# A fused hybrid-mixer and mixture-of-experts layer: the fourth head's projection order, its output-weight split, and the products of the recurrence's first and last step

## What is computed

```python
def step(S, inp):
    qg_c, kd_c, u_c, w_c, intra_c, a_c = inp
    v_new = u_c - jnp.einsum('bhik,bhkv->bhiv', w_c, S)
    o_c = (jnp.einsum('bhik,bhkv->bhiv', qg_c, S)
           + jnp.einsum('bhij,bhjv->bhiv', intra_c, v_new))
    S = S * a_c[..., None, None] + jnp.einsum('bhik,bhiv->bhkv', kd_c, v_new)
    return S, o_c
S0 = jnp.zeros((B, H, DK, DV), q.dtype)
_, o = lax.scan(step, S0, xs)
```

## Time and profile before

| what | us |
|---|---|
| median of 3 runs | 1310.05 |
| profiled execution | 1305.95 |
| its span, first to last instruction | 1304.1 |
| TensorE busy | 1246.6 (96% of the span) |
| head 3, from its gk round (462.43) to the end of rz6 | 72.61 |
| the same stretch of head 2 (337.46) | 60.38 |

### The profile page before, as it was taken

How to read it: one execution, slowest core, us unless ns; L and a number is a source line. 1 busy time by engine, 2 the same in 40 slices (tenths; PEclk the granted TensorE clock), 3 DMA queues, 4 the chain that set the end, 5 groups by cost and what they waited for, 6 DMA issues and landing times.

```text
span 1304.1 us, 25780 instructions
## 1 busy us (share of the span) xinstructions
PE 1246.6 (96%) x10894; PEld 1075.7 (82%) x10894; DVE 896.9 (69%) x1085; ACT 722.7 (55%) x919; POOL 174.1 (13%) x144
## 2 busy tenths in 40 slices
PE   7999999999999997899978999999999999999977
PEld 6989899989999997678877888888888888888854
DVE  7655457445655554324457889888989899889867
ACT  7351336133413432433235788878887878888834
POOL 0020111021102010600011111111111111111000
PEclk9999999999999998899988999999999999999998
DMA  7101010111010103045417999999999999999986
GB/s 212 50 17 36 18 46 21 36 34 33 29 27 31 33 18 131 2 189 182 178 50 278 375 377 392 383 390 394 395 386 378 394 385 390 388 381 384 371 333 256
DMA packets 38217, 273.98 MB, mean 210 GB/s; under 512 B 8163, under 2 KB 8419, under 8 KB 25844
## 3 DMA queue, kind: packets, MB, share of 16 engines
q1 hardware_dynamic: 28484, 251.67, 51.2%
q0 software_dynamic: 9216, 16.80, 3.4%
q10 hardware_dynamic: 432, 4.27, 0.9%
HBM read 260.11 MB, written 29.36 MB: 222 GB/s over the span
## 4 chain that ended last, share of the span: by engine, by line
PE 87%; DVE 7%; issue 2%; DMA 2%; ACT 2%; SPq 0%; DVEq 0%; POOLq 0%
PE bank L602 13%; PE bank L604 13%; PE bank L603 13%; PE bank L1317 8%; PE bank L1319 8%; PE bank L1318 8%; PE bank L489 2%; PE bank L493 2%; PE bank L491 2%; PE bank L593 2%; DVE arena L1887 1%; PE bank L1433 1%; PE bank L621 1%; PE bank L1460 1%; PE bank L1463 1%
## 5 line engine op out<-in xcount | busy, mean ns | idle before, releaser
L968 DVE TENSOR_TENSOR w_lo<-w_raw,w_hi 128x2048 fp32r<-128x2048 f32 x192 | 432.6, 2285 | 39.0 <-ACT w_hi L749 38.2
L749 ACT ACTIVATE w_hi<-w_raw 128x2048 fp32r<-128x2048 f32 x192 | 360.6, 1916 | 71.6 <-DMA w_raw<-in_w_up 46.8
L1317 PE MATMUL bank<-xn_hi,p_hi 128*128 128x364 f32 (+1 forms) x672 | 230.4, 343 | 4.8 <-DVE xn_lo L1834 2.5
L1319 PE MATMUL bank<-xn_hi,p_lo 128*128 128x364 f32 (+1 forms) x672 | 216.0, 321 | 0.0
L1318 PE MATMUL bank<-xn_lo,p_hi 128*128 128x364 f32 (+1 forms) x672 | 215.7, 321 | 0.0
L602 PE MATMUL bank<-w_hi,xgT_hi 128*128 128x512 f32 x512 | 206.3, 403 | 2.9 <-DVE xgT_lo L1026 2.9
L604 PE MATMUL bank<-w_hi,xgT_lo 128*128 128x512 f32 x512 | 201.4, 393 | 0.0
L603 PE MATMUL bank<-w_lo,xgT_hi 128*128 128x512 f32 x512 | 200.9, 392 | 0.0
L1317 PEld LDWEIGHTS bank<-xn_hi,p_hi 128*128 128x128 f32 x672 | 127.0, 189 | 7.7 <-DVE xn_lo L1834 2.8
L1318 PEld LDWEIGHTS bank<-xn_lo,p_hi 128*128 128x128 f32 x672 | 127.2, 189 | 0.3
L1319 PEld LDWEIGHTS bank<-xn_hi,p_lo 128*128 128x128 f32 x672 | 126.8, 189 | 0.0
(11 more groups left out here) (268 smaller groups left out, 1890.4 us busy)
## 6 DMA issues: line engine op xcount, KB each, us to landing
w_raw<-in_w_down SPq DMA_DIRECT2D x32, 2048.0 KB, 10.0
w_raw<-in_w_gate SPq DMA_DIRECT2D x31, 2048.0 KB, 10.9
w_raw<-in_w_up SPq DMA_DIRECT2D x31, 2048.0 KB, 9.9
p_raw<-in_w_tiles SPq DMA_DIRECT2D x28, 512.0 KB, 3.6
arena<-y_rows SPq DMA_DIRECT2D x8, 1024.0 KB, 13.7
arena<-in_tokens SPq DMA_DIRECT2D x10, 416.0 KB
w_out_raw<-in_w_out SPq DMA_DIRECT2D x4, 1024.0 KB, 9.4
arena<-in_tokens SPq DMA_DIRECT2D x8, 512.0 KB, 4.5
```

The lines of the kernel that those rows point to most:

```text
L749: nc.scalar.activation(w_hi[m][:, half], wraw[m if raw is None else raw][:, half], ACT.Copy).then_inc(hi_done[m], 1)
L968: nc.vector.tensor_tensor(w_lo[m][:, half], wraw[m if raw is None else raw][:, half], w_hi[m][:, half].bitcast(F32), ALU.subtract).then_in ...
L1317: nc.tensor.matmul(out[:, 0:n], p_hi[slot][:, k, :], hi, start=(k == 0), stop=False)
L1319: m = nc.tensor.matmul(out[:, 0:n], p_lo[slot][:, k, :], hi, start=False, stop=(k == KD - 1))
```

## The change

Four edits:

1. Head 3 gets the order of projection pieces of the other heads, on TensorE and VectorE. Its splits of y stand at other rounds.
2. `w_out` is therefore read later in the head (the wait for the last GB piece is the same). The split of its eight blocks is spread: two high parts on ScalarE behind ttr5, two behind the "mix" norm, four in steps 0 to 3; low parts of blocks 0, 2, 5, 3 on GpSimd, and of 1, 4, 6, 7 on VectorE.
3. The recurrence leaves out, in step 0, the products with the zero state (L1493, L1500) and VectorE's r, takes bv in r's place, and copies the first state; in step 9 it leaves out the product and the update of a state that nobody reads. The state's memset goes.
4. The gaps of a step are filled by `step_fill`: heads 0 to 2 get the next head's first Z piece in the gaps of step 9 (1, 2 and 5 of its 8 blocks) instead of behind it; head 3 gets its 18 units in steps 1 to 9, and none before the recurrence or in step 0.

```diff
+        HI_ORDER, LO_POOL, LO_DVE = [0, 1, 2, 4, 5, 6, 3, 7], [0, 2, 5, 3], [1, 4, 6, 7]
@@ TensorE
+            STEP_TILES = ([{1: range(2, 5), 2: range(5, 8)}] + [{0: range(0, 3), 1: range(3, 5), 2: range(5, 8)}] * (NC - 2)
+                          + [{0: range(0, 1), 1: range(1, 3), 2: range(3, 8)}])
             def scan(h, last):
-                if last:
-                    early_pair(0, 0)
-                else:
+                if not last:
                     fill(h, Q, 0, range(0, 2))
...
+                def step_fill(c, third):
+                    if last and c:
+                        early_pair(c - 1, third)
+                    if not last and third in STEP_TILES[c]:
+                        if c < NC - 1:
+                            fill(h, Q + c // 3, c % 3, STEP_TILES[c][third])
+                        else:
+                            fill(h + 1, Z, 0, STEP_TILES[c][third])
...
+                    if c:
+                        pe.wait_ge(s_done, h * (NC - 1) + c)
+                        nc.tensor.matmul(bank[3][0:C, 0:128], chunk(kT, c), state, start=True, stop=True).then_inc(ks_done, 1)
+                        step_fill(c, 0)
+                        if c >= 2:
+                            pe.wait_ge(osq_done, h * NC + c - 1)
+                        nc.tensor.matmul(o, state, chunk(qg, c), start=True, stop=False)
+                        pe.wait_ge(r_done, h * (NC - 1) + c)
+                    nc.tensor.matmul(bank[4][0:C, 0:128], rT[0:C, c, :], r_sb[0:C, :] if c else bv[0:C, 0, :],
                                      start=True, stop=True).then_inc(vnp_done, 1)
+                    step_fill(c, 1)
                     pe.wait_ge(vn_done, h * NC + c + 1)
+                    m = nc.tensor.matmul(o, vn_sb[0:C, :], dTi[0:C, c, :], start=(c == 0), stop=True)
+                    if c < NC - 1:
+                        m = nc.tensor.matmul(bank[6][:, 0:128], kd[0:C, c, :], vn_sb[0:C, :], start=True, stop=True)
+                    m.then_inc(ods_done, 1)
+                    step_fill(c, 2)
...
-                if last:
-                    fills = {"z1": [(GC, 2), (UU, 0)], "rz1": [(UU, 1), (UU, 2)], "z2": [(GB, 0), (GB, 1)], "rz2": [(GB, 2)]}
-                else:
-                    fills = {...}
+                fills = {"z1": [(GC, 2)], "rz1": [(UU, 0)], "ttr1": [(UU, 1, LOW)], "z2": [(UU, 1, HIGH)],
+                         "rz2": [(UU, 2, LOW)], "ttr2": [(UU, 2, HIGH)], "z3": [(GB, 0, LOW)], "rz3": [(GB, 0, HIGH)],
+                         "ttr3": [(GB, 1, LOW)], "z4": [(GB, 1, HIGH)], "rz4": [(GB, 2)]}
...
-                fill(h + 1, Z, 0)
                 scan_end(h)
@@ ScalarE
+                    if last and n == 3:
+                        early_high(2)
+                    if last and n == 4:
                         early_high(0)
-                    if last and n >= 3:
-                        for k in ((0, 1), (2, 3, 4), (5, 6, 7))[n - 3]:
...
+                    if last and n == 5:
+                        w_out_high(0)
+                        w_out_high(1)
                 log_exp_tables()
                 norm(h, "mix", 1.0 / 64, eps)
+                if last:
+                    w_out_high(2)
+                    w_out_high(3)
                 for c in range(NC):
                     act.wait_ge(vnp_done, h * NC + c + 1)
                     nc.scalar.activation(vn_sb[0:C, :], bank[4][0:C, 0:128], ACT.Copy).then_inc(vn_done, 1)
+                    if last and c < 4:
+                        w_out_high(c + 4)
@@ VectorE, in the recurrence
+                    if last and c in (1, 2, 5):
+                        w_out_low({1: 4, 2: 6, 5: 7}[c])
...
+                    if c == 0:
+                        nc.vector.tensor_copy(state, bank[6][:, 0:128]).then_inc(s_done, 1)
@@ GpSimd
+                    w_out_low(0)
+                    w_out_low(2)
...
                 for c in range(NC):
+                    if last and c in (1, 4):
+                        w_out_low(5 if c == 1 else 3)
```

More of the change, by code:

```diff
@@ L1491, in scan @@
                     o = bank[(5, 7)[c % 2]][:, 0:C]
[L1492 to L1499, removed]
@@ L1503, in scan @@
+                    nc.tensor.matmul(bank[4][0:C, 0:128], rT[0:C, c, :], r_sb[0:C, :] if c else bv[0:C, 0, :],
                                      start=True, stop=True).then_inc(vnp_done, 1)
[L1504 to L1507, removed]
+                    step_fill(c, 1)
                     pe.wait_ge(vn_done, h * NC + c + 1)
-                    nc.tensor.matmul(o, vn_sb[0:C, :], dTi[0:C, c, :], start=False, stop=True)
@@ L2039, in mixer @@
                 grp(h, "z1")
-                if last:
[L2041 to L2047, removed]
-                    early_low(1)
[L2049 to L2073, removed]
+                grp(h, "rz1")
+                u_piece(0)
+                grp(h, "z2")
+                lo_part(0, use(h, GB))
+                grp(h, "rz2")
+                if last:
+                    early_low(1)
+                u_piece(1)
+                grp(h, "z3")
+                u_piece(2)
+                grp(h, "rz3")
+                mix_conv()
+                gb_piece(0)
+                grp(h, "z4")
+                gb_piece(1)
+                grp(h, "rz4")
+                gb_piece(2)
                 if not last:
                     lo_part(SLOT[Q], use(h, Q))
+                if last:
+                    early_low(2)
                 for n in (5, 6):
@@ L2078, in mixer @@
                     grp(h, f"rz{n}")
+                    if last and n == 5:
+                        early_low(0)
+                if last:
+                    w_out_low(1)
                 if not last:
@@ L2112, in mixer @@
                 if not last:
-                    dve.wait_ge(s_done, h * (NC + 1) + NC + 1)
+                    dve.wait_ge(s_done, (h + 1) * (NC - 1))
                     head_copies(h + 1)
@@ L2139, in _, with w_out_low @@
             g_incl(0)
+            def w_out_low(k):
+                pool.wait_ge(wo_hi_done, HI_ORDER.index(k) + 1)
+                nc.gpsimd.tensor_tensor(w_out_lo[:, k, :], w_out_raw[:, k, :], w_out_hi[:, k, :].bitcast(F32),
+                                        ALU.subtract).then_inc(wo_lo_done, 1)
             def mixer(h, last):
@@ L2152, in mixer @@
                 if last:
-                    for k in range(KD):
-                        pool.wait_ge(wo_hi_done, k + 1)
-                        nc.gpsimd.tensor_tensor(w_out_lo[:, k, :], w_out_raw[:, k, :], w_out_hi[:, k, :].bitcast(F32),
-                                                ALU.subtract).then_inc(wo_lo_done, 1)
+                    w_out_low(0)
+                    w_out_low(2)
                 if not last:
```

41 lines of the change are left out of this document (22 added, 19 removed).

## The result

The changed kernel takes 1289.96 us (median of 5 runs, 1286.68 to 1293.68) against 1310.31 us (5 runs, 1308.07 to 1312.9): ratio 0.984, 95% interval 0.982 to 0.986, so 20.4 us less. The profiled execution took 1287.59 (span 1285.7) against 1305.95 (1304.1), 18.4 less, and that difference can be followed through the trace. The other 2.0 lie between the medians and the two profiled executions, and no trace shows them. By the interval of the ratio the changed kernel takes 1286.5 to 1292.5, so the run itself doesn't place it clearly outside the range.

What follows compares the result with a forecast made beforehand. It took TensorE to bound the kernel, idle or low-clocked in head 3. Gains 7.2 and 12.2 less 2.0 (gate), 0.2 (rest of head 3), 1.0 (port), 2.0 (clock) gave 14.2 us: 1296, range 1290.5 to 1301.5.

Steps and rivals of the forecast that it cites:

- Heads 0 to 2: Recurrence steps 0 and 9: dropped products and the Z fill save 2.4 us a head, 7.2 for three.
- Head 3's preparation: Head 3, gk round to rz6: with head 2's order it takes head 2's time, 12.2 us saved.
- instructions not yet there: Reading of TensorE's "issue" waits, up to 4.05 us, in head 3's dense small rounds beside a saturated DMA.
- Gate: Head 3, rz6 to step 1: output-weight landing and ScalarE's splits delay the recurrence, 7.1 us instead of 5.1, loss 2.0.
- against what I listed: Expected sign ahead of head 3's recurrence: ScalarE waits about 1 us for DMA before the first weight split.
- Clock: Head 3 near step 0: idle TensorE's clock falls to 0.50 for about 5 us, loss 2.0, ends 0 and 4.
- Port: Head 3, steps 1, 2 and 4: GpSimd and VectorE splits block each other, loss 1.0 us, ends 0 and 3.
- so I let a shift of head 3's end pass to the end unchanged: Behind head 3: output and expert products follow, so time gained there reaches the kernel's end in full.
- the experts' span unchanged: Expected sign behind head 3: the experts take as long as before the change.

Runs made afterwards that it cites:

- warm: The kernel gate plus 14 dummy products of 384 columns in TensorE's gaps ahead of step 0 and in steps 0 and 1; 1291.85 us, ratio 0.985.
- gate: The changed kernel with ScalarE's output-weight splits moved behind the first vn copies and early output products a step later; 1287.35 us, ratio 0.983.
- best: The kernel warm plus 17 float32 dummy products of 8 columns ahead of the first load's landing; 1288.04 us, ratio 0.981.

## Why the prediction was right, and where it failed

**Heads 0 to 2:** 7.2 forecast, 7.55 measured. The shares differ: dead products alone 1.5, Z beside step 9 1.05 once they are gone. Head 2's preparation gained waits on issue of 0.59 and 1.14 (gk to rz6 60.79 instead of 59.54), for which I had no term.

**Head 3's preparation:** 12.2 forecast, 12.5 measured. Reading it off head 2 was right, and "instructions not yet there" as the meaning of issue was right. What I blamed, the saturated DMA, is the smaller part: the transfer's place is worth 5.4, the order 8.7. The Trainium skill's "mostly hidden" (Runtime: NRT & Kernel Launch, "Instruction fetch mechanics"), which I set against the trace, does not hold in dense rounds: 3.75 us a block.

**Gate:** +2.0 forecast, +1.5 measured, as the first quarter landed after 5.2 us and ScalarE's first split followed the last copy of ttr5 directly; it didn't wait for DMA, against what I listed.

**Clock:** +2.0 forecast, +1.9 measured. The clock lay at 0.50 from about 517.7 to 527.9, twice the 5 us forecast (and the fall in the earlier trace rows that the forecast leans on came at 1269.2, after 3.6 us of idleness, not 4); the first half of that TensorE mostly waited, so the price is near all the same. Step 1 took 4.78, the others 2.8 to 2.9, and the one with the mix output 3.78 (3.70 before). The dummies in warm confirm the cause: with the clock at 1.00, 2.2 us less than gate. They don't confirm the size: gate is another arrangement, and 2.0 us of waits for VectorE stand in warm's steps.

**Port:** 1.0 forecast, at most 0.1 measured: steps 1 to 9 lost 1.88, all of it in the one slow step. GpSimd's longest split grew to 3.59, but nothing on the path waited for it. That was the order in which the two engines happened to start: in gate VectorE's splits grew from 1.2 to 1.7 and 1.9, in steps that also had the low clock, and in warm, at the full clock, to 2.2 to 2.6, where TensorE waited 2.0 us for them. So the term was sized within its ends of 0 and 3, and was 0 here by luck as much as by argument.

**The step that failed:** "so I let a shift of head 3's end pass to the end unchanged", and with it "the experts' span unchanged". The stretch to the last expert's block gave back 1.9, and the closing stage gave 5.4 more. The wait of 5.54 was among my rows, and I used it only to learn how the clock behaves. A wait on issue has no releaser whose timing could be followed, but it depends on where the program's blocks of instructions end, and the change took 24 recorded products out. The experiments price it at 4.3 us: 1296 - 4.3 is 1291.7, inside the range.

**Open:** the 1.9 us given back in the experts. 1.0 of it is one wait for VectorE (1.63 at 1232.78 where before had 0.66 at 1245.77); over the kernels that stretch varies by some 4 us with no order that I could find, and nothing was tried on it. Also open: the stand ends 3.2 to 3.6 us after its block has come, in the rounds a wait ends 1.2 to 1.5 after; whether the skipped loop body ahead of the stage makes the difference was not tried.

## What to carry to other kernels

Take every wait on issue as a term of its own: any edit that changes the number of an engine's instructions can remove it or bring it, far from where the edit is. Put long products between dense rounds of small ones, so that their instructions arrive in time, and keep bulk transfers off these rounds. When a sound edit gives nothing, look for such a wait before throwing it away: warm and best differ by 17 idle products and, in the medians, 3.8 us. The page's instruction queue, read in narrow windows, tells whether a wait on issue is a wait for a block.

## What the runs showed of the hardware

- In dense rounds, at the granted clock of 0.50, TensorE got 128 products with their weight loads per 3.75 us with the DMA idle, and per 6.2 us with it saturated. Each wait ended 1.2 to 1.5 us after a 16 KB block of the instruction queue.
- Programs with 10884, 10894 or 11022 recorded products in all had a stand of 3.8 to 5.5 us at the same place, ending 3.2 to 3.6 us after such a block; with 10870, 10918 and 10958 there was none.
- A product of plain float32 operands shows as two recorded products; one of the rounded high and low parts shows as one (warm's 14 dummies: 14 more).
- A VectorE subtraction with two operands in SBUF took 1.21 us alone and 2.24 to 2.60 beside GpSimd's in warm; in the changed kernel it was GpSimd's that grew, from 2.36 to 3.59.
- Fourteen products of 384 columns held the clock at 1.00 through a stretch in which it otherwise lay at 0.50 for some ten microseconds.
